# Position bias of a neighbourhood-attention block read as shifted strips of padded, reversed rows instead of a scattered grid in DRAM

## What is computed

```
mod = silu(c) @ ada_w + ada_b          # shift, scale and gate vectors
h   = modulate(rms_norm(x), sh1, sc1)  # then one wide projection: q, k, v and gates
```

```
s_win = q . k * scale + rpb[h, key_row - row + 7, key_col - col + 15]
p     = softmax([s_win, s_ctx])        # window keys and all context keys in one softmax
```

## Time and profile before

| | |
|---|---|
| median of three runs | 1817.05 us |
| span of the profiled execution | 1811.3 us |
| what lies around the span (median less span) | 5.75 us |
| PE busy | 1734.9 us (96%) |
| DVE busy | 1165.6 us (64%) |
| ACT busy | 816.7 us (45%) |
| POOL busy | 117.8 us (7%) |
| moved by DMA | 372.68 MB |

### The profile page before, as it was taken

The page is one execution under the profiler, slowest core; times in us unless marked ns, Lnnn a source line. Parts: engine busy times, 40 slices in busy tenths (PEclk is TensorE's granted clock), DMA queues, the critical chain, the costliest instruction groups (busy, mean ns, idle before and its releaser), DMA issues.

```text
span 1811.3 us, 23692 instructions
## 1 busy us (share of the span) xinstructions
PE 1734.9 (96%) x8663; PEld 1447.0 (80%) x8663; DVE 1165.6 (64%) x1434; ACT 816.7 (45%) x1011; POOL 117.8 (7%) x170
## 2 busy tenths in 40 slices
PE   5899899989999989999999999999999999999997
PEld 3578678878788857888888878888888888888885
DVE  5775676887776597455455566666666666655556
ACT  4864112461222456444444455555555555544443
POOL 0002322133221000000000000000000000000000
PEclk9899999999999999999999999999999999999998
DMA  9889888828886422655656546555555655555551
GB/s 365 313 271 233 294 292 278 289 60 309 286 278 230 129 70 82 226 192 186 196 186 214 192 142 191 190 187 189 192 186 189 192 186 193 186 190 196 192 191 69
DMA packets 153516, 372.68 MB, mean 206 GB/s; under 512 B 11788, under 2 KB 12429, under 8 KB 152558
## 3 DMA queue, kind: packets, MB, share of 16 engines
q1 hardware_dynamic: 132160, 296.18, 48.8%
q0 software_dynamic: 20720, 75.43, 13.1%
q10 hardware_dynamic: 574, 0.25, 0.1%
HBM read 367.73 MB, written 5.03 MB: 206 GB/s over the span
## 4 chain that ended last, share of the span: by engine, by line
PE 83%; DMA 6%; DVE 6%; ACT 2%; issue 1%; SPq 0%; DVEq 0%; POOLq 0%; ACTq 0%
PE ps L1582 20%; PE ps L1581 10%; PE ps L1591 10%; PE ps L1593 10%; PE ps L1592 10%; DMA ada_raw<-in_ada_w 4%; PE ps L1892 4%; PE ps L1893 4%; PE ps L1894 4%; DMA raw<-in_ada_w 2%; PE ps L1487 2%; PE ps L1498 1%; PE ps L1578 1%; DVE ada_acc L996 1%; PE ps L1500 1%
## 5 line engine op out<-in xcount | busy, mean ns | idle before, releaser
L930 DVE TENSOR_TENSOR w_lo<-raw,w_hi 128x1024 fp32r<-128x1024 f32 x552 | 670.0, 1223 | 500.7 <-ACT w_hi L564 499.2
L564 ACT CAST w_hi<-raw 128x1024 fp32r<-128x1024 f32 x552 | 576.0, 1049 | 918.2 <-PE ps L1593 339.0
L1582 PE MATMUL ps<-h2T,w_hi 128*128 128x512 f32 x1320 | 462.5, 394 | 0.0
L1581 PE MATMUL ps<-h2T,w_lo 128*128 128x256 f32 x1320 | 366.5, 278 | 0.0
L1582 PEld LDWEIGHTS ps<-h2T,w_hi 128*128 128x128 f32 x1320 | 247.5, 188 | 53.5
L1581 PEld LDWEIGHTS ps<-h2T,w_lo 128*128 128x128 f32 x1320 | 247.9, 188 | 4.0
L996 DVE SCALAR_TENSOR_TENSOR ada_acc<-ada_raw,silu_c,ada_acc 128x512 f32<-128x512 f32 x240 | 180.0, 750 | 49.5 <-DMA ada_raw<-in_ada_w 30.8
L1591 PE MATMUL ps<-w_hi,hT 128*128 128x512 f32 x512 | 201.4, 393 | 1.9 <-DVE mod L1005 1.9
L1593 PE MATMUL ps<-w_hi,hT 128*128 128x512 f32 x512 | 200.2, 391 | 0.0
L1592 PE MATMUL ps<-w_lo,hT 128*128 128x512 f32 x512 | 199.9, 390 | 0.0
L1892 PE MATMUL ps<-w_hi,f_hi 128*128 128x512 f32 x352 | 137.0, 389 | 1.0 <-DVE conv_in L1328 1.0
(11 more groups left out here) (214 smaller groups left out, 2084.0 us busy)
## 6 DMA issues: line engine op xcount, KB each, us to landing
raw<-in_ffn_w_up SPq DMA_DIRECT2D x176, 512.0 KB, 4.4
raw<-in_w_in SPq DMA_DIRECT2D x160, 512.0 KB, 4.5
ada_raw<-in_ada_w POOLq DMA_DIRECT2D x128, 512.0 KB, 6.1
raw<-in_ffn_w_down SPq DMA_DIRECT2D x88, 512.0 KB, 3.5
raw<-in_ada_w SPq DMA_DIRECT2D x64, 512.0 KB, 5.8
raw<-in_w_out SPq DMA_DIRECT2D x32, 512.0 KB, 3.6
raw<-in_w_branch_a SPq DMA_DIRECT2D x16, 512.0 KB, 3.5
raw<-in_w_branch_b SPq DMA_DIRECT2D x16, 512.0 KB, 3.5
```

The costliest lines, as they stand in the source:

```text
L564: act.copy(w_hi[:, s % SPLIT_SLOTS, :], raw[:, s, :]).then_inc(hi_ready[s], 1)
L930: dve.tensor_tensor(w_lo[:, s % SPLIT_SLOTS, :], raw[:, s, :], w_hi[:, s % SPLIT_SLOTS, :], ALU.subtract).then_inc(lo_ready[s], 1)
L1581: pe.matmul(ps[:, b + t, 0:SEQ], w_lo[:, row4(s), at], high(kc), start=False, stop=False)
L1582: mm = pe.matmul(o, w_hi[:, row4(s), at], both(kc), start=False, stop=(kc == KC - 1))
```

## The change

The grid in DRAM, its clearing and its scatter go. POOL now loads the 120 rows of 31 numbers into SBUF at the very start, copies them in reversed order into the middle of cleared rows of 128 numbers (`pad_rows`) and stores these to DRAM (`rpb_pad`, 61 KB). Read from element p on, 64 numbers of such a row are the bias of query column p in reversed key order. One DMA takes 64 such strips (one a partition) of six rows each: six rows of distance cover all four key rows of both query rows with the same parity. A head needs two DMAs of 96 KB in place of four of 64 KB. They land in a single buffer `bias_in`. DVE's mask add reads it backwards and writes `bias`, 384 numbers a partition in place of 512; a half then takes its 256 numbers from an offset. The loads of head h now wait until the mask add of head h - 1 is done (`bias_ready`), and the mask add of head h waits for both loads.

```diff
-            pool.memset(zeros[:], 0.0).then_inc(zeros_ready, 1)
+            pool.memset(pad_rows[:], 0.0).then_inc(zeros_ready, 1)
             pool.dma_start(lam_in[:], diff_lambda...)
...
+            pool.wait_ge(zeros_ready, 1)
+            pool.dma_start(rpb_rows[:], na_rpb[0].rearrange("h r w -> (h r) w")).then_inc(rpb_landed, 16)
+            pool.wait_ge(rpb_landed, 16)
+            pool.tensor_copy(pad_rows[:, PAD_AT:PAD_AT + RPB_COLS], rpb_rows[:, ::-1]).then_inc(zeros_ready, 1)
+            pool.wait_ge(zeros_ready, 2)
+            pool.dma_start(rpb_pad.ap(), pad_rows[:]).then_inc(padded, 16)
+
             pool.wait_ge(mod_cols_ready, 2)
-            pool.wait_ge(zeros_ready, 1)
-            pool.dma_start(rpb_grid.ap().rearrange("p (a n) -> p a n", a=ZERO_PARTS),
-                           zeros[:].unsqueeze(1)
-                           .to_broadcast([HEADS * RPB_ROWS, ZERO_PARTS, RPB_BLOCK // ZERO_PARTS]))\
-                .then_inc(padded, 16)
-
-            def scatter_bias(pair):
-                if pair == ADA_SLOTS - 1:
-                    pool.wait_ge(padded, 16)
-                    pool.dma_start(bass.AP(rpb_grid, RPB_MARGIN - (WIN_COLS - 1),
-                                           [[RPB_BLOCK, HEADS * RPB_ROWS], [GRID_W + 1, GRID_W], [1, RPB_COLS]]),
-                                   na_rpb[0].rearrange("h r w -> (h r) w").unsqueeze(1)
-                                   .to_broadcast([HEADS * RPB_ROWS, GRID_W, RPB_COLS])).then_inc(padded, 16)
-
-            load_ada(0, skip_wait=True, between=scatter_bias)
-            pool.wait_ge(padded, 32)
+            load_ada(0, skip_wait=True)
+            pool.wait_ge(padded, 16)

-            def load_bias(h, r):
-                src = bass.AP(rpb_grid, (h * RPB_ROWS + WIN_ROWS - 1 - r) * RPB_BLOCK + RPB_MARGIN,
-                              [[GRID_W, GRID_W], [RPB_BLOCK, ROWS], [1, GRID_W]])
...
+            def load_bias(h, odd):
+                src = bass.AP(rpb_pad, (h * RPB_ROWS + WIN_ROWS - ROWS + 1 - odd) * PAD_ROW,
+                              [[1, GRID_W], [PAD_ROW, NEAR], [1, GRID_W]])
+                dst = bias_in[odd * GRID_W:(odd + 1) * GRID_W, :].rearrange("p (a b) -> p a b", a=NEAR)
+                pool.dma_start(dst, src).then_inc(bias_landed, 16)
...
-            for h in range(2, HEADS):
-                pool.wait_ge(na_biased, TOK * (h - 1))
-                for r in range(ROWS):
-                    load_bias(h, r)
+            for h in range(1, HEADS):
+                pool.wait_ge(bias_ready, h)
+                for odd in range(2):
+                    load_bias(h, odd)
...
                 if t == 0:
-                    dve.wait_ge(bias_landed[h % 2], 64 * (h // 2 + 1))
-                    b = bias[:, h % 2, :].rearrange("p (a b) -> p a b", b=GRID_W)
-                    dve.tensor_tensor(b, b, mask, ALU.add).then_inc(bias_ready, 1)
+                    dve.wait_ge(bias_landed, 32 * (h + 1))
+                    near = bias_in[:].rearrange("p (a b) -> p a b", b=GRID_W)[:, :, ::-1]
+                    dve.tensor_tensor(bias[:].rearrange("p (a b) -> p a b", b=GRID_W), near, mask, ALU.add)\
+                        .then_inc(bias_ready, 1)
...
                 dve.scalar_tensor_tensor(scores[:, n % 3, 0:SEQ], ps[:, n % 2, 0:SEQ], NA_SCALE,
-                                         bias[:, h % 2, t * SEQ:(t + 1) * SEQ], ALU.mult, ALU.add)\
+                                         bias[:, 2 * (1 - t) * GRID_W:(2 * (1 - t) + ROWS) * GRID_W],
+                                         ALU.mult, ALU.add)\
```

More of the change, by code:

```diff
@@ L35 @@
 RPB_COLS = 2 * WIN_COLS - 1
-RPB_MARGIN = WIN_COLS
-RPB_BLOCK = GRID_W * GRID_W + 2 * RPB_MARGIN
-ZERO_PARTS = 8
+PAD_ROW = 2 * GRID_W
+PAD_AT = GRID_W - 1 - (WIN_COLS - 1)
+NEAR = ROWS + 2
 MAP_DIM = 64
@@ L168, in block_program @@
     qT = place("qT", arena + 32 * kb, [P, HEADS, SEQ])
-    bias = place("bias", arena + 40 * kb, [P, 2, TOK * SEQ])
+    bias_in = place("bias_in", arena + 40 * kb, [P, NEAR * GRID_W])
     diff_pT = place("diff_pT", arena + 40 * kb, [P, 2, 2 * TOK, P])
@@ L232, in block_program @@
     lam_prod = place("lam_prod", lat + 9 * kb, [P, 2, MAP_DIM])
-    zeros = place("zeros", arena + 40 * kb, [HEADS * RPB_ROWS, RPB_BLOCK // ZERO_PARTS])
+    bias = place("bias", arena + 42 * kb, [P, NEAR * GRID_W])
+    rpb_rows = place("rpb_rows", arena + 41 * kb, [HEADS * RPB_ROWS, RPB_COLS])
+    pad_rows = place("pad_rows", arena + 40 * kb, [HEADS * RPB_ROWS, PAD_ROW])
     ident = consts[:, C_IDENT:C_IDENT + P]
-    rpb_grid = nc.dram_tensor("rpb_grid", [HEADS * RPB_ROWS, RPB_BLOCK], F32)
+    rpb_pad = nc.dram_tensor("rpb_pad", [HEADS * RPB_ROWS, PAD_ROW], F32)
     ps = nc.alloc_psum_tensor("ps", [P, 8, GROUP], F32)
@@ L289, in block_program @@
         zeros_ready = sem("zeros_ready")
+        rpb_landed = sem("rpb_landed")
         padded = sem("padded")
-        bias_landed = sems("bias_landed", 2)
+        bias_landed = sem("bias_landed")
         bias_ready = sem("bias_ready")
@@ L517, in _ @@
-            load_ada(0, skip_wait=True, between=scatter_bias)
-            pool.wait_ge(padded, 32)
-            def load_bias(h, r):
-                src = bass.AP(rpb_grid, (h * RPB_ROWS + WIN_ROWS - 1 - r) * RPB_BLOCK + RPB_MARGIN,
-                              [[GRID_W, GRID_W], [RPB_BLOCK, ROWS], [1, GRID_W]])
-                dst = bias[(r % 2) * GRID_W:(r % 2 + 1) * GRID_W, h % 2,
-                           (r // 2) * SEQ:(r // 2 + 1) * SEQ].rearrange("p (a b) -> p a b", a=ROWS)
-                pool.dma_start(dst, src).then_inc(bias_landed[h % 2], 16)
@@ L528, in load_first_biases @@
-            def load_first_biases(pair):
-                load_bias(pair // ROWS, pair % ROWS)
+            pool.wait_ge(zeros_ready, 1)
[4 more added lines that the diff above has]
+            pool.dma_start(rpb_pad.ap(), pad_rows[:]).then_inc(padded, 16)
@@ L532, in _, with load_first_bias @@
+            def load_first_bias(pair):
+                if pair < 2:
+                    load_bias(0, pair)
             pool.wait_ge(hT_ready, KC)
-            load_ada(1, between=load_first_biases)
+            load_ada(1, between=load_first_bias)
             with pool.Fori(2, ADA_BEFORE_NA) as g:
                 load_ada(g)
-            for h in range(2, HEADS):
-                pool.wait_ge(na_biased, TOK * (h - 1))
-                for r in range(ROWS):
-                    load_bias(h, r)
+            for h in range(1, HEADS):
+                pool.wait_ge(bias_ready, h)
+                for odd in range(2):
+                    load_bias(h, odd)
@@ L1087, in _ @@
                 split_lo(JOB_DIFF, s)
-            mask = consts[:, C_MASK:C_MASK + GRID_W].unsqueeze(1).to_broadcast([P, TOK * ROWS, GRID_W])
+            mask = consts[:, C_MASK:C_MASK + GRID_W].unsqueeze(1).to_broadcast([P, NEAR, GRID_W])
             def na_bias(n):
```

## The result

The changed kernel takes 1798.49 us (median of 4 runs, 1798.35 to 1801.59); the kernel before, 1816.4 us (median of 4, 1814.90 to 1817.54). The ratio is 0.9898, 95% interval 0.9881 to 0.9915: faster by about 1%, 18 us. The stall went as predicted. The size did not come as predicted, and the sections that follow are mostly about why.

A forecast was written before the change was run, and what follows sets the result against it. PE, busy 96% of a 1811.3 us span, was taken as the bound. Terms -9.7 - 3.8 + 0.2 - 0.1 + 0 = -13.4 us, off the median 1817.05, gave 1803.6 us; range 1801.5 to 1806, or to 1809 with rival A.

The forecast's parts named there:

- What bounds the kernel, and what goes: Jobs 9 and 10: PE sets the time; its scatter-caused stalls with slow clock go, gaining 9.7 and 3.8 us.
- the two waits: PE's waits of 7.38 us in job 9 and 1.92 us in job 10, priced with slow clock at 9.7 and 3.8.
- DMA or DVE late next: Stretch after the stall: neither takes the scatter's place; demand 285 GB/s against 279 moved, DVE 10 us ahead of PE.
- Rival A: Job 10: the stall shrinks but DVE stays late and the second wait stays; gain 9.6 us, 1807.4; chance 0.07.
- The preparation at the start: Head, first 10 us: loading 15 KB and storing 61 KB beside the head's weights costs at worst 0.3 us, counted +0.2.
- The mask add: Attention, DVE: 384 numbers take 0.55 us, 0.13 us a head less; counted -0.1 us.
- the backward read: DVE's mask add: assumed no dearer than forward; if twice as long a number, 0.95 us and 1.1 us in all.
- The loop: Attention's single-buffer refill: wake, issue, landing and mask add take 3.9 us against PE's 4.54 a head; free, counted 0.
- the 1.8 us of a longer issue: Attention: DVE's scaling could delay the second load's issue by 0.49 us; loop 4.8 us, cost 1.8 us, 1805.4 in all.
- B: Attention: the single-buffer loop binds mildly, landing in 3.5 to 4.5 us; costs 4 to 11 us, 1808 to 1814; chance 0.09.
- C: Attention: overlapping strip loads are truly slow, landing in 7.4 us; costs 32 us, time 1835; chance 0.03.
- The span is 5.75 us below the median of the runs, and I keep this.: Whole kernel: the 5.75 us gap was kept, so 13.4 us came off the median 1817.05, giving 1803.6.

The follow-up runs named there:

- the third profile: Another profiled execution of the unchanged kernel before: scatter 35.9 us, PE's wait in job 9 11.7 us, span 1812.3 us.
- second and fourth of the kernel before: Two further profiled executions of the unchanged kernel before: scatter 36.1 and 37.6 us, spans 1817.7 and 1820.1 us.

## Why the prediction was wrong

*What bounds the kernel, and what goes.* Right: the scatter held up DVE's loads, DVE held up `w_lo`, PE ran dry. That these loads were late because they stood behind the scatter on its queue is not shown, since the weight loads on SP's queue took as long. In the changed kernel PE waits nowhere in jobs 9 to 13 and the clock stays at 1.00. PE's first score multiply comes at 348.38 us, before at 362.38. That is 14.0 us, of which 0.3 come from the head; predicted was 13.5 us for the two waits, and 13.7 came.

*DMA or DVE late next.* Right for the stretch: 275 GB/s at 0.83 with PE full. Rival A did not come.

*The preparation at the start:* +0.2 predicted, not seen; PE's last transposes of the head start at 158.1 in place of 158.5. In the four profiles of the kernel before this point lies anywhere from 157.3 to 160.5, so 0.2 us could not be seen.

*The mask add:* 0.55 us, exactly as worked out. All eight are 550 to 558 ns, so the backward read costs nothing that shows; the Trainium skill's rule on the plain mode (VectorE: DVE Perf Modes, Mode 1× (REGULAR) — the baseline) agrees with the trace.

*The loop:* 4.3 us against 3.9. A load of 96 KB lands in 2.8 us, not 2.42: by spreading the 16% of DMA time over the loads I priced half as many bytes again at 0.12 us, and 0.5 came. Bytes and runs grow together here (384 runs in place of 256), so which of them costs it is open. It stayed free, with one DVE wait of 0.27 us. The issues take 662 to 664 ns, and the 1.8 us of a longer issue did not come. The scaling L1121 falls beside them, but mostly starts 0.53 us into the second issue, and neither gets longer then. Where it starts earlier, one of the two does. It starts 0.12 us into three issues of the kernel before, and these took 754 to 757 ns in place of 617 (the 757 of the earlier trace rows); in the kernel with the scatter put back and in the one with two early loads it starts 0.16 and 0.17 us into one issue, which took 886 and 897 ns. Where it starts 0.34 us into an issue of the changed kernel, twice, the scaling takes longer, 0.54 and 0.58 us in place of 0.49. That one of the two waits for the other agrees with the port rule of the Trainium skill (SBUF — State Buffer, Who interferes with whom); when POOL takes the port within its issue, no row shows. Rivals B and C did not come; the experiment with four loads shows that B priced a loop longer than PE's 4.54 us rightly.

*The step that failed: "The span is 5.75 us below the median of the runs, and I keep this."* The difference was not time around the span, which is 1.6 to 2.0 us in every run that lists both, but one of 3.25 us. It was some 4 us by which the profiled execution was faster than the usual one. Of the 53 executions of the kernel before that were timed for the experiments one had a span as short as 1811.3 us, and the median span was 1817.6. Taken against its own time, estimated as 1811.3 + 1.7 = 1813.0, the sum gives 1813.0 - 13.4 = 1799.6 us, 1.1 above the median measured. By adding the gap to the forecast I had the changed kernel keep a loss that the change removes: the other three profiles have a scatter of 36 to 38 us and a PE wait of 12 to 14, not 7.4, and their jobs 9 to 13 take 2.3, 4.5 and 7.0 us more than the first profile's, about the 5 us that were missing. Not all of the gap is this loss: beyond job 13 the spans also differ by low clock and by the wait in job 15, and the third profile comes out short by them. Why the scatter takes 31 us in one execution and 38 in another is open. The three runs before the change lay at 1815.8 to 1817.5, and a span of 1811.3 was the hint.

*The rest.* Between the two first profiles 14.9 us went, not 13.4. The attention took 1.3 us more, since the clock fell behind PE's wait of 2.4 us at its start, as it had not in the first profile before. Then job 15 took 3.3 us less (a wait of 0.4 in place of 2.2, and no low clock), and the differential attention's start 1.2 us more, again by low clock. Why the clock falls behind a wait in one execution and not in another, nothing here settles.

## What to carry to other kernels

A profile is one execution. Before a stall is priced by it, compare its span with the spread of the times; a gap of several microseconds that the program's start and end don't explain may be the stall's own variation, and a change that removes the stall removes that too. A DMA of thousands of short runs delays the loads behind it on its queue and those of other queues too; price it by the landings of the loads issued while it runs and not by its bytes, and follow the delay on: the engine that waited may be late at later meetings even where the first one is covered. A single buffer that is refilled on release is free only while wake, issue, landing and use fit into the bound engine's period; take the landing from a load of the same size where there is one.

## What the runs showed of the hardware

- 7680 runs of 124 bytes to DRAM took 31.2, 35.9, 36.1 and 37.6 us in four executions of one program; 480 runs of 1984 bytes, the same 930 KB, 10.7 us. During the first, the DMA engines were 94% busy at 92 GB/s, and loads of 512 KB issued meanwhile landed in 22 to 27 us on SP's queue and in 25 on POOL's, against 3.8 to 8.7 and 4.0 to 7.2 us in the changed kernel (issued from 160 to 190 us).
- Reading the source from SBUF in place of DRAM, in runs as short, left it at 32.8 us.
- A load of 384 runs of 256 bytes landed in 2.6 to 3.0 us in the attention, one of 256 such runs in 2.2 to 2.7. The first start at every fourth byte and overlap; what that costs is inside the difference.
- A VectorE float32 add with one operand read backwards took 550 to 558 ns for 384 numbers a partition, the 0.55 us worked out from forward reads of 512 and 1024.
- A DMA issue of POOL took 754 to 757 ns in place of 617 when a VectorE float32 scaling of 0.49 us began 0.12 us into it, 886 and 897 in place of 664 when it began at 0.16 and 0.17 us. Begun 0.34 us into an issue of 662 to 664 ns, the scaling itself took 0.54 and 0.58 us.
- PE's wait of 2.4 to 2.6 us at the attention's start was followed by low clock in both profiles of the changed kernel (0.73 from 355 to 360 us in the first) and in the second and fourth of the kernel before, but not in its first and third.
